# Two output norms: gain moved from the rows of W_out, and 1/rms from the accumulator add, onto the activations

## The chip, the cores and the metric

The kernel runs on one core of a Trainium2 chip. The metric is the device time of one execution in microseconds (us), the median of several. The core has a matrix engine (TensorE, PE in the rows; PEld is its weight load), VectorE (DVE), ScalarE (ACT), GpSimd (POOL) and SyncE (SP), which here only issues DMAs. PE writes to PSUM; the other compute engines read it, GpSimd excepted.

## The reference

```python
for i in range(DEPTH):                                     # DEPTH is 1
    proj = rmsnorm(h, norm_mix_g[i]) @ w_in[i]
    y_a = gmlp_chunk_mixer(proj[..., :GM_COLS], ...)       # ends: rmsnorm((u * mixed), gm_out_norm_g), width 1024
    y_b = ssd_mixer(proj[..., GM_COLS:], ...)              # ends: y * silu(z), then rmsnorm with ssd_norm_g,
                                                           #       two groups of 512 columns
    h = h + jnp.concatenate([y_a, y_b], axis=-1) @ w_out[i]
    hid = jax.nn.relu(rmsnorm(h, norm_mlp_g[i]) @ w_ff1[i])
    h = h + (hid * hid) @ w_ff2[i]
    gate = jax.nn.sigmoid(rmsnorm(h, ple_norm_g[i]) @ w_ple_gate[i])
    h = h + gate * (p[i] @ w_ple_proj[i])
return rmsnorm(h, final_norm_g)
```

x is 512 x 1024, everything is float32. The change touches the two rmsnorms that end `y_a` and `y_b`, and the product with `w_out` behind them.

## The kernel before

The 512 positions are four row tiles of 128. Every large product is made of three TensorE passes: both operands are split into a float32r high part and the rest (`w_hi`, `w_lo`, `a_hi`, `a_lo`, `b_hi`, `b_lo`), and high x high, high x low, low x high are added in PSUM. A weight block of 512 columns (or, for `w_out`, of four 128-row slices over all 1024 columns) arrives in `w_raw` by four DMAs of 512 KB from SyncE's queue, ACT rounds each piece to `w_hi` (L594), DVE subtracts to get `w_lo` (L989 or L991).

The first part runs through 36 steps t = 4 b + s: block b of `w_in` (v: 0, 1; the convolved columns: 2 to 4; u: 5, 6; z: 7, 8) against row tile s, 24 matmuls each. The order on each engine is written by hand as one loop over t, with semaphores between the engines, and work of other kinds is put at certain t. From t = 20 the state-space scan runs beside it, one unit j per two steps (j = 0 to 7, two groups of four chunks). Unit j needs: PE the product `cb` at odd t (L1615), DVE its mask and the product `lm` at even t (L1084, L1088), PE `off`, `diag` and `state` at even t (L1623, L1628, L1635), GpSimd the three products `xdt`, `xdd` and `y *= d_skip` after them (L541, L544, L548), then DVE at the following odd t the sum (L1151 to L1167). These small products go to four PSUM banks, `side`, filled in a fixed order. Bank 3 takes cb 6, off 6, cb 7, off 7: so `cb` of unit 7, which PE has behind its matmuls of t = 33, waits until DVE has read `off` of unit 6 in L1151, at t = 33 of DVE's own order.

`u * mixed` is multiplied in place in `h` (L1226, t = 20 to 27), its squares are summed by ACT (L791), and at t = 32 DVE takes the reciprocal of the rms (L1177, into `m_rstd`). PE turns `h` to `a_hi`/`a_lo` from t = 34 on (`yt` parts 0 and 1). `y * silu(z)` is multiplied in place in `y` (L1232, t = 28 to 35) and turned at t = 40 to 43 (`yt` parts 2 and 3).

The product with `w_out` is blocks OUT to OUT + 3 (b = 9 to 12, t = 36 to 51), 24 matmuls a tile into two PSUM banks, and DVE adds each finished tile to `h` (L1045), into which x has been read once more. Neither norm is applied to the activations: the gains of both norms are read as 16 rows of `rows`, turned to columns 68 to 83 of `cols`, and multiply the rows of `w_out` when it is split (L594 with `scale`, L989); `m_rstd` multiplies in the add (L1045), one column a row tile for y_a and for each group of y_b. After that come the PLE product, the feed-forward product (a seven-product scheme) and the gate.

The buffer `gain` has two slots of 1024 columns, each filled by a DMA that spreads a row of 4 KB over 128 partitions.

Of the kernel before, what the change touches and what calls it, by code (L numbers as in the profile page):

```python
# [5 lines left out]
P = 128  # L6
# [22 lines left out]
def build_layer(nc, a, out):  # L29
# [26 lines left out]
    with ExitStack() as ctx:  # L56
# [66 lines left out]
        rows = sb("rows", [P, P])  # L123
        cols = sb("cols", [P, 84])
        a_log = sb("a_log", [P, R])
# [66 lines left out]
        m_ssq_ready, m_rms_ready = sem("m_ssq_ready"), sem("m_rms_ready")  # L192
        m_rstd_ready = sem("m_rstd_ready")
        yt_hi, pt_hi = sem("yt_hi"), sem("pt_hi")
        f1_landed = [[sem(f"f1_landed{i}{p}") for p in range(2)] for i in range(3)]
# [140 lines left out]
        def _(sp):  # L336
# [38 lines left out]
            sp.dma_start(rows[60:68, :], a["gm_bs"][0]).then_inc(rows_landed, 16)  # L375
            sp.dma_start(rows[68:76, :], a["gm_out_norm_g"][0].rearrange("(i p) -> i p", p=P)).then_inc(rows_landed, 16)
            sp.dma_start(rows[76:84, :], a["ssd_norm_g"][0].rearrange("(i p) -> i p", p=P)).then_inc(rows_landed, 16)
            sp.dma_start(y[:, 0:1, :].rearrange("p a (g s) -> p (a g) s", g=GH),
# [9 lines left out]
            sp.wait_ge(xn_ready, NS)  # L388
            load_gain(a["norm_mlp_g"][0], 0)
            load_k(U, w_in, 0)  # L390
            load_k(U + 1, w_in, 512)
            for i in range(2):
                load_k(Z + i, w_in, 2 * W + 512 * i)
            load_rows(OUT, w_out, 0)
            load_rows(OUT + 1, w_out, 4)
            sp.wait_ge(m_ssq_ready, 4)
            for s in range(NS):
# [4 lines left out]
            sp.dma_start(tmp[:, 0:2, :].rearrange("p a (b n) -> p (a b) n", b=2), p_dram).then_inc(p_landed, 16)  # L402
            load_rows(OUT + 3, w_out, 12)
            for p in range(4):
                piece(PLE, p, w_ple[:, p // 2, 512 * (p % 2):512 * (p % 2) + 512], w_raw[:, p, 0, :])
# [175 lines left out]
        def _(act):  # L581
            def split_hi(b, p):

                half = b % 2 if b < GATE else 1 - b % 2
                act.wait_ge(w_landed[p], 16 * (b + 1))
                if b == GATE:
                    act.wait_ge(ff_step, product_end(UNITS - 1, "T4"))
                elif b > GATE:
                    act.wait_ge(ff_step, STEPS * UNITS)
                elif b >= 2:  # L590
                    act.wait_ge(acc_full, 4 * (b - 1))
                n = 1 if b == PLE else 2
                scale = cols[:, 68 + 4 * (b - OUT) + p:69 + 4 * (b - OUT) + p] if OUT <= b < PLE else 1.0
                act.activation(w_hi[:, half, 2 * p:2 * p + n, :], w_raw[:, p, 0:n, :], ACT.Copy, scale=scale  # L594
                               ).then_inc(hi_ready, 1)

# [382 lines left out]
        def _(dve):  # L979
            def split_lo(b, p):  # L980

                half = b % 2 if b < GATE else 1 - b % 2
                dve.wait_ge(hi_ready, 4 * b + p + 1)
                n = 1 if b == PLE else 2
                lo, raw = w_lo[:, half, 2 * p:2 * p + n, :], w_raw[:, p, 0:n, :]
                hi = w_hi[:, half, 2 * p:2 * p + n, :].bitcast(F32)
                if OUT <= b < PLE:
                    c = 68 + 4 * (b - OUT) + p
                    ins = dve.scalar_tensor_tensor(lo, raw, cols[:, c:c + 1], hi, ALU.mult, ALU.subtract)  # L989
                else:  # L990
                    ins = dve.tensor_tensor(lo, raw, hi, ALU.subtract)  # L991
                ins.then_inc(lo_ready, 1)

            def normed(n, s):

                i = 4 * n + s
                dve.wait_ge(rms_ready, i + 1)
                dve.reciprocal(rstd[:, i:i + 1], rms[:, i:i + 1]).then_inc(rstd_ready, 1)
                dve.wait_ge(rstd_ready, i + 1)
                slot, use = ((0, 1), (0, 2), (1, 2))[n]  # L1000
                c = s if n < 2 else TILES[s]
                if s == 0:
                    dve.wait_ge(gain_landed[slot], 16 * use)
                if n == 0:
                    dst = h[:, s, :]
                else:
                    dst = tmp[:, 2 * (s % 2):2 * (s % 2) + 2, :].rearrange("p a n -> p (a n)")
                dve.scalar_tensor_tensor(dst, h[:, c, :], rstd[:, i:i + 1], gain[:, slot, :], ALU.mult, ALU.mult
                                         ).then_inc(xn_ready, 1)
# [24 lines left out]
            def add_group(b, s):  # L1034

                dve.wait_ge(acc_full, 4 * b + s + 1)
                if b == OUT:
                    dve.wait_ge(x_landed[s], 32)
                else:
                    prev = before[b] + s + 1 - 4  # L1040
                    dve.wait_ge(dve_evac, prev)
                i = 2 * (s % 2)
                hs = h[:, s, :].rearrange("p (a n) -> p a n", a=2)
                c = 4 * max(b - OUT - 1, 0) + s
                dve.scalar_tensor_tensor(hs, acc[:, i:i + 2, :], m_rstd[:, c:c + 1], hs, ALU.mult, ALU.add  # L1045
                                         ).then_inc(dve_evac, 1)

# [43 lines left out]
            for t in range(4 * OUT):  # L1091
# [12 lines left out]
                if t == 3:  # L1104
                    bank = wait_full(dve, "cols")
                    freed(dve.tensor_copy(cols[:], bank[:, 0:84]), "cols")
                if t == 4:
# [67 lines left out]
                if t == 32:  # L1175
                    dve.wait_ge(m_rms_ready, 1)
                    dve.reciprocal(m_rstd[:, 0:4], m_rms[:, 0:4]).then_inc(m_rstd_ready, 1)  # L1177
                    dve.wait_ge(m_rstd_ready, 1)
                if t == 19:
                    mask_cb(0)  # L1180
# [53 lines left out]
            def yb_scale(g):  # L1234
# [3 lines left out]
                dve.reciprocal(m_rstd[:, at], m_rms[:, at]).then_inc(m_rstd_ready, 1)  # L1238
                dve.wait_ge(m_rstd_ready, 2 + g)


# [187 lines left out]
            for i in range(8):  # L1429
# [14 lines left out]
                if i == 0:  # L1444
                    dve.wait_ge(gain_landed[0], 16 * 3)
                dve.tensor_tensor(y[:, s, at], h[:, s, at], gain[:, 0, at], ALU.mult).then_inc(h_gain, 1)
# [11 lines left out]
        def _(pe):  # L1458
# [95 lines left out]
            for t in range(4 * OUT):  # L1554
# [5 lines left out]
                if t == 2:  # L1560
                    pe.wait_ge(rows_landed, 16 * 5)
                    filled(pe.transpose(open_bank("cols")[:, 0:84], rows[0:84, :], ident[0:84, 0:84]), "cols")
                if t == 4:
# [73 lines left out]
                if t >= 34:  # L1637
                    if t == 34:
                        pe.wait_ge(ya_mul, 8)
                    for k in (2 * (t - 34), 2 * (t - 34) + 1):  # L1640
# [3 lines left out]
            for b in range(OUT, OUT + 4):  # L1644
                for s in range(4):
# [14 lines left out]
                    if 40 <= t < 44:  # L1660
                        i = t - 40
                        pe.wait_ge(yb_mul, 5 + i)
                        for q in range(2):
# [131 lines left out]
```

## Time and profile before

| what | us |
|---|---|
| median of 3 runs | 754.24 |
| the runs | 754.21, 754.24, 755.58 |
| the profiled execution, device time | 755.58 |
| its span, first to last instruction | 753.8 |
| PE busy in it | 736.7 (98%) |
| DVE / ACT / POOL busy | 460.3 / 379.9 / 116.8 |

The profiled execution is the slowest of the three. In its rows, a matmul of 512 columns is shown with 0.39 us and the next begins 0.23 us after it, so a step of 24 takes about 5.5 us. Times of rows are us from the start of the span. A row's first number is its start, the second how long it took; "idle before" stands in brackets with what ended it.

### The profile page before, as it was taken

The numbers are of one execution on the slowest core, as the hardware profiler recorded it, in microseconds if no ns is written. First come the engines' busy times: TensorE is split into PE (matmuls) and PEld (weight loads), VectorE is DVE, ScalarE is ACT, GpSimd is POOL, SyncE is SP. The second block draws the span as 40 slices with busy tenths as digits, with TensorE's granted clock in tenths as the row PEclk, the third lists the DMA queues.
The fourth block names the chain that finished last, engine by engine and source line by source line (L and its number), as shares of the span: only waits on it lengthen the run. The fifth ranks groups of instructions, "written<-read, shape, count | busy, mean of one in ns | idle before, by whom it ended". The sixth has DMA issues, their size and how long they took to land.

```text
span 753.8 us, 8663 instructions
## 1 busy us (share of the span) xinstructions
PE 736.7 (98%) x3396; PEld 606.7 (80%) x3396; DVE 460.3 (61%) x492; ACT 379.9 (50%) x508; POOL 116.8 (15%) x92
## 2 busy tenths in 40 slices
PE   7999999999999999999999999999999999998896
PEld 7888877878878888888888888888888888886784
DVE  5557885576767465546454952586356844498854
ACT  5534456654674833314564523563257326554665
POOL 1021310766455000000002000110002000200000
PEclk9999999999999999999999999999999999999998
DMA  9632222352241163101967694477727681883311
GB/s 336 183 102 85 83 84 86 116 163 85 86 159 63 59 216 116 57 29 36 383 195 166 154 275 130 112 148 245 221 52 155 194 270 56 167 215 125 109 57 56
DMA packets 48001, 106.10 MB, mean 141 GB/s; under 512 B 4677, under 2 KB 6361, under 8 KB 47961
## 3 DMA queue, kind: packets, MB, share of 16 engines
q1 hardware_dynamic: 41096, 84.55, 33.5%
q0 software_dynamic: 5632, 16.78, 12.3%
q10 hardware_dynamic: 1232, 4.23, 1.9%
q8 instruction: 27, 0.44, 0.2%
q14 instruction: 14, 0.11, 0.0%
HBM read 88.73 MB, written 4.23 MB: 123 GB/s over the span
## 4 chain that ended last, share of the span: by engine, by line
PE 89%; DVE 7%; ACT 1%; issue 1%; DMA 1%; SPq 0%; DVEq 0%; ACTq 0%
PE acc L1469 26%; PE acc L1471 25%; PE acc L1470 25%; PE side L1531 3%; PE side L1628 2%; PE side L1470 1%; PE side L1471 1%; PE side L1469 1%; DVE ring_lo L1275 1%; DVE w_lo L991 1%; DVE h L1347 1%; PE side L1595 1%; DVE conv L1188 1%; DVE h L1332 1%; PE side L1635 1%
## 5 line engine op out<-in xcount | busy, mean ns | idle before, releaser
L1469 PE MATMUL acc<-w_hi,a_hi 128*128 128x512 f32 x256 | 104.3, 408 | 0.0
L1471 PE MATMUL acc<-w_hi,a_lo 128*128 128x512 f32 x256 | 100.0, 391 | 0.0
L1470 PE MATMUL acc<-w_lo,a_hi 128*128 128x512 f32 x256 | 99.7, 390 | 0.0
L1469 PE MATMUL acc<-b_hi,ring_hi 128*128 128x512 f32 x256 | 99.6, 389 | 0.0
L1470 PE MATMUL acc<-b_lo,ring_hi 128*128 128x512 f32 x256 | 99.6, 389 | 0.0
L1471 PE MATMUL acc<-b_hi,ring_lo 128*128 128x512 f32 x256 | 99.6, 389 | 0.0
L991 DVE TENSOR_TENSOR w_lo<-w_raw,w_hi 128x1024 fp32r<-128x1024 f32 (+1 forms) x48 | 67.2, 1409 | 31.7 <-ACT w_hi L594 31.3
L662 ACT ACTIVATE ring_hi<-quarter 128x1024 fp32r<-128x1024 f32 x56 | 56.5, 1051 | 51.1 <-PE acc L1471 31.4
L1275 DVE TENSOR_TENSOR ring_lo<-ring_raw,ring_hi 128x1024 fp32r<-128x1024 f32 x32 | 38.7, 1224 | 67.0 <-ACT ring_hi L662 66.8
L1275 DVE TENSOR_TENSOR ring_lo<-quarter,ring_hi 128x1024 fp32r<-128x1024 f32 x56 | 65.9, 1219 | 16.8 <-ACT ring_hi L662 16.8
L571 POOL DMA_DIRECT2D quarter<-quarter x24 | 20.8, 868 | 351.4 <-DMA quarter<-in_w_ff 223.7
L662 ACT ACTIVATE ring_hi<-ring_raw 128x1024 fp32r<-128x1024 f32 x32 | 33.8, 1057 | 60.3 <-DMA ring_raw<-in_w_ff 60.2
L1469 PEld LDWEIGHTS acc<-w_hi,a_hi 128*128 128x128 f32 x256 | 48.1, 188 | 10.8 <-issue 1.4
L1470 PEld LDWEIGHTS acc<-w_lo,a_hi 128*128 128x128 f32 x256 | 48.2, 188 | 10.7 <-issue 1.4
L1471 PEld LDWEIGHTS acc<-w_hi,a_lo 128*128 128x128 f32 x256 | 48.0, 188 | 10.4
L594 ACT ACTIVATE w_hi<-w_raw 128x1024 fp32r<-128x1024 f32 (+1 forms) x48 | 48.1, 1013 | 16.0 <-PE acc L1471 13.7
L1469 PEld LDWEIGHTS acc<-b_hi,ring_hi 128*128 128x128 f32 x256 | 48.1, 188 | 10.0
L1470 PEld LDWEIGHTS acc<-b_lo,ring_hi 128*128 128x128 f32 x256 | 48.1, 188 | 9.9
L1471 PEld LDWEIGHTS acc<-b_hi,ring_lo 128*128 128x128 f32 x256 | 48.1, 188 | 9.9
L1469 PE MATMUL acc<-w_hi,b_hi 128*128 128x512 f32 x128 | 50.6, 396 | 4.1 <-DVE b_lo L1020 4.1
L1471 PE MATMUL acc<-w_hi,b_lo 128*128 128x512 f32 x128 | 49.9, 390 | 0.0
L1470 PE MATMUL acc<-w_lo,b_hi 128*128 128x512 f32 x128 | 49.8, 389 | 0.0
(228 smaller groups left out, 1460.5 us busy)
## 6 DMA issues: line engine op xcount, KB each, us to landing
quarter<-in_w_ff SPq DMA_DIRECT2D x40, 512.0 KB, 4.8
w_raw<-in_w_in SPq DMA_DIRECT2D x36, 512.0 KB, 3.8
ring_raw<-in_w_ff SPq DMA_DIRECT2D x32, 512.0 KB, 5.4
quarter<-quarter POOLq DMA_DIRECT2D x24, 512.0 KB, 6.1
w_raw<-in_w_out SPq DMA_DIRECT2D x16, 512.0 KB, 3.5
h<-in_x SPq DMA_DIRECT2D x8, 512.0 KB, 4.4
seg<-cs_dram ACTq DMA_DIRECT2D x8, 512.0 KB, 3.8
quarter<-in_w_ff POOLq DMA_DIRECT2D x8, 512.0 KB, 6.6
```

The costliest lines, as they stand in the source:

```text
L571: pool.dma_start(quarter[QUARTER[name]][at], src, accum_op=ALU.add).then_inc(t_landed[QUARTER[name]][p], 16)
L594: act.activation(w_hi[:, half, 2 * p:2 * p + n, :], w_raw[:, p, 0:n, :], ACT.Copy, scale=scale).then_inc(hi_ready, 1)
L662: act.activation(hi[at], src, ACT.Copy).then_inc(form_hi, 1)
L991: ins = dve.tensor_tensor(lo, raw, hi, ALU.subtract)
L1188: ins = dve.scalar_tensor_tensor(dst, acc[:, s, 0:SEQ - k], w, dst, ALU.mult, ALU.add)
L1275: dve.tensor_tensor(lo[at], src, hi[at].bitcast(F32), ALU.subtract).then_inc(form_lo, 1)
L1332: dve.tensor_tensor(hq, hq, bank, op).then_inc(h_added, 1)
L1469: pe.matmul(dst, st[0], mv[0], start=start, stop=False)
L1470: pe.matmul(dst, st[0], mv[1], start=False, stop=False)
L1471: return pe.matmul(dst, st[1], mv[0], start=False, stop=stop)
L1531: ins = pe.transpose(bank[:, i * P:i * P + P], src(i), ident[:])
L1628: ins = pe.matmul(bank[:, r * HD:r * HD + HD], lm[:, r, :], xdt[:, r * HD:r * HD + HD], start=True, stop=True)
```

## The change

- The two gains are no longer read into `rows`; `cols` has 68 columns. W_out is split like every other weight: L594 without `scale`, a plain subtraction for `w_lo`.
- At t = 32, behind the reciprocal, DVE multiplies the four row tiles of `h` (1024 columns each) by 1/rms and gain, four new instructions, in place. It raises `ya_norm`; PE waits for it before it turns `h` at t = 34.
- At t = 37 and t = 39, in `yb_scale`, DVE does the same with four half tiles of `y` (512 columns) each, eight new instructions. They raise `yb_norm`; PE waits for it at t = 40 to 43.
- The add of a finished tile is a plain sum `h + acc`.
- SyncE's queue: gain slot 0 takes `gm_out_norm_g` where it took `norm_mlp_g`; slot 1 takes `ssd_norm_g` after a wait for `v_ready`, ahead of block U + 1; `norm_mlp_g` follows after a wait for `ya_norm`, ahead of block OUT + 1. The wait for `m_ssq_ready` ahead of the second read of x goes; the PLE pieces wait for `yb_norm`.

```diff
-            sp.dma_start(rows[68:76, :], a["gm_out_norm_g"][0].rearrange("(i p) -> i p", p=P)).then_inc(rows_landed, 16)
-            sp.dma_start(rows[76:84, :], a["ssd_norm_g"][0].rearrange("(i p) -> i p", p=P)).then_inc(rows_landed, 16)
...
             sp.wait_ge(xn_ready, NS)
-            load_gain(a["norm_mlp_g"][0], 0)
+            load_gain(a["gm_out_norm_g"][0], 0)
             load_k(U, w_in, 0)
+            sp.wait_ge(v_ready, NS)
+            load_gain(a["ssd_norm_g"][0], 1)
             load_k(U + 1, w_in, 512)
...
             load_rows(OUT, w_out, 0)
+            sp.wait_ge(ya_norm, NS)
+            load_gain(a["norm_mlp_g"][0], 0)
             load_rows(OUT + 1, w_out, 4)
-            sp.wait_ge(m_ssq_ready, 4)
...
-                scale = cols[:, 68 + 4 * (b - OUT) + p:69 + 4 * (b - OUT) + p] if OUT <= b < PLE else 1.0
-                act.activation(w_hi[:, half, 2 * p:2 * p + n, :], w_raw[:, p, 0:n, :], ACT.Copy, scale=scale
-                               ).then_inc(hi_ready, 1)
+                act.activation(w_hi[:, half, 2 * p:2 * p + n, :], w_raw[:, p, 0:n, :], ACT.Copy).then_inc(hi_ready, 1)
...
-                if OUT <= b < PLE:
-                    c = 68 + 4 * (b - OUT) + p
-                    ins = dve.scalar_tensor_tensor(lo, raw, cols[:, c:c + 1], hi, ALU.mult, ALU.subtract)
-                else:
-                    ins = dve.tensor_tensor(lo, raw, hi, ALU.subtract)
-                ins.then_inc(lo_ready, 1)
+                dve.tensor_tensor(w_lo[:, half, 2 * p:2 * p + n, :], w_raw[:, p, 0:n, :],
+                                  w_hi[:, half, 2 * p:2 * p + n, :].bitcast(F32), ALU.subtract).then_inc(lo_ready, 1)
...
-                c = 4 * max(b - OUT - 1, 0) + s
-                dve.scalar_tensor_tensor(hs, acc[:, i:i + 2, :], m_rstd[:, c:c + 1], hs, ALU.mult, ALU.add
-                                         ).then_inc(dve_evac, 1)
+                dve.tensor_tensor(hs, hs, acc[:, i:i + 2, :], ALU.add).then_inc(dve_evac, 1)
...
                     dve.wait_ge(m_rstd_ready, 1)
+                    dve.wait_ge(gain_landed[0], 32)
+                    for i in range(NS):
+                        dve.scalar_tensor_tensor(h[:, i, :], h[:, i, :], m_rstd[:, i:i + 1], gain[:, 0, :],
+                                                 ALU.mult, ALU.mult).then_inc(ya_norm, 1)
...
                 dve.wait_ge(m_rstd_ready, 2 + g)
+                dve.wait_ge(gain_landed[1], 32)
+                for i in range(NS):
+                    yv = y[:, i, 512 * g:512 * g + 512]
+                    dve.scalar_tensor_tensor(yv, yv, m_rstd[:, 4 + 4 * g + i:5 + 4 * g + i],
+                                             gain[:, 1, 512 * g:512 * g + 512], ALU.mult, ALU.mult).then_inc(yb_norm, 1)
...
-                        pe.wait_ge(ya_mul, 8)
+                        pe.wait_ge(ya_norm, NS)
...
-                        pe.wait_ge(yb_mul, 5 + i)
+                        pe.wait_ge(yb_norm, 5 + i)
```

VectorE at t = 32 and 33, before: the mask product of unit 6, the first piece of `w_out`, the reciprocal, the product with silu(z), the second piece, and the read of `off` (bank `side`).

```order
161 L1088 TENSOR_TENSOR lm<-lm,cbm 128x1024
162 L989 SCALAR_TENSOR_TENSOR w_lo<-w_raw,cols,w_hi 128x1024
163 L1177 RECIPROCAL m_rstd<-m_rms 128x4
164 L1232 TENSOR_TENSOR y<-y,tmp 128x512
165 L989 SCALAR_TENSOR_TENSOR w_lo<-w_raw,cols,w_hi 128x1024
166 L1151 TENSOR_TENSOR xs_t<-side,decay 128x512
```

The same stretch with the change (the lines have moved: L1144 is what L1151 was, L1229 what L1232 was).

```order
161 L1081 TENSOR_TENSOR lm<-lm,cbm 128x1024
162 L986 TENSOR_TENSOR w_lo<-w_raw,w_hi 128x1024
163 L1170 RECIPROCAL m_rstd<-m_rms 128x4
164 L1174 SCALAR_TENSOR_TENSOR h<-h,m_rstd,gain 128x1024 x4
165 L1229 TENSOR_TENSOR y<-y,tmp 128x512
166 L986 TENSOR_TENSOR w_lo<-w_raw,w_hi 128x1024
167 L1144 TENSOR_TENSOR xs_t<-side,decay 128x512
```

Four instructions of 1024 columns now stand between the reciprocal and everything up to the read of `off`.

VectorE at t = 37 to 40, before: adds of finished tiles, with the reciprocals of the y_b norm between them.

```order
188 L1045 SCALAR_TENSOR_TENSOR h<-acc,m_rstd,h 128x1024
189 L1238 RECIPROCAL m_rstd<-m_rms 128x4
190 L989 SCALAR_TENSOR_TENSOR w_lo<-w_raw,cols,w_hi 128x1024
191 L1045 SCALAR_TENSOR_TENSOR h<-acc,m_rstd,h 128x1024
```

With the change:

```order
189 L1039 TENSOR_TENSOR h<-h,acc 128x1024
190 L1235 RECIPROCAL m_rstd<-m_rms 128x4
191 L1240 SCALAR_TENSOR_TENSOR y<-y,m_rstd,gain 128x512 x4
192 L986 TENSOR_TENSOR w_lo<-w_raw,w_hi 128x1024
193 L1039 TENSOR_TENSOR h<-h,acc 128x1024
```

Four instructions of 512 columns come between the reciprocal and the next piece of weights; the same stands once more at t = 39.

## Rows read from the trace of the kernel before

**Rows 1.** The page: busy us by engine, and the granted clock in tenths by slice.

```profile
PE 736.7 (98%) x3396; PEld 606.7 (80%) x3396; DVE 460.3 (61%) x492; ACT 379.9 (50%) x508; POOL 116.8 (15%) x92
...
PEclk9999999999999999999999999999999999999998
```

**Rows 2.** Waits of PE: who for whom, us in total, times, longest us.

```profile
PE acc L1469 <- DVE b_lo L1020: 4.1, 2, 2.4
...
PE side L1531 <- ACT xs_t L833: 1.1, 2, 0.8
```

**Rows 3.** Timeline, DVE, 228 to 256 us: start, us, what.

```profile
235.26 0.17 DVE L1177 RECIPROCAL m_rstd<-m_rms 128x4 f32<-128x4 f32 x1
235.85 0.69 DVE L1232 TENSOR_TENSOR y<-y,tmp 128x512 f32<-128x512 f32 x1 [0.42 <-DVE m_rstd L1177]
236.84 1.28 DVE L989 SCALAR_TENSOR_TENSOR w_lo<-w_raw,cols,w_hi 128x1024 fp32r<-128x1024 f32 x1 [0.29 <-ACT w_hi L594]
238.04 0.68 DVE L1151 TENSOR_TENSOR xs_t<-side,decay 128x512 f32<-128x512 f32 x1
238.75 1.40 DVE L1156 TENSOR_TENSOR xs_t<-xs_t,y 128x512 f32<-128x512 f32 x1
...
240.79 0.81 DVE L1165 TENSOR_TENSOR carry<-carry,decay 128x512 f32<-128x512 f32 x1
241.64 0.69 DVE L1167 TENSOR_TENSOR carry<-side,carry 128x512 f32<-128x512 f32 x1
...
247.01 1.23 DVE L1088 TENSOR_TENSOR lm<-lm,cbm 128x1024 f32<-128x1024 f32 x1 [1.49 <-ACT lm L707]
```

**Rows 4.** Timeline, POOL, 222 to 256 us, the three instructions of unit 7.

```profile
238.56 1.04 POOL L541 TENSOR_TENSOR xdt<-y,dt 128x512 f32<-128x512 f32 x1 [6.42 <-PE side L1635]
239.68 1.37 POOL L544 TENSOR_TENSOR xdd<-xdt,decay 128x512 f32<-128x512 f32 x1
241.02 1.49 POOL L548 TENSOR_TENSOR y<-y,d_skip 128x512 f32<-128x512 f32 x1
```

**Rows 5.** Timeline, PE: `cb` and `diag` of unit 7, and the turn of `h`.

```profile
243.74 0.38 PE L1615 MATMUL side<-bcT 128*128 128x128 f32 x2
...
250.31 1.89 PE L1628 MATMUL side<-xdt,lm 128*128 128x64 f32 x16
252.04 1.04 PE L1531 MATMUL side<-ident,h 128*128 128x128 f32 x8
```

**Rows 6.** Timeline, DVE, 160 to 170 us, an instruction of 1024 columns beside POOL.

```profile
160.52 1.78 DVE L1088 TENSOR_TENSOR lm<-lm,cbm 128x1024 f32<-128x1024 f32 x1 [1.37 <-ACT lm L707]
```

**Rows 7.** Timeline, POOL, the instruction that ran beside it.

```profile
158.48 2.74 POOL L529 TENSOR_TENSOR seg<-seg,upper 128x1024 f32<-128x1024 f32 x1
```

**Rows 8.** Groups by line and form, DVE: busy us, mean ns, idle before.

```profile
L1008 DVE SCALAR_TENSOR_TENSOR tmp<-h,rstd,gain 128x1024 f32<-128x1024 f32 x8 | 10.3, 1284 | 0.3
...
L1188 DVE SCALAR_TENSOR_TENSOR conv<-acc,cols,conv 128x511 f32<-128x511 f32 x12 | 8.9, 745 | 10.1 <-ACT conv L824 10.1
```

**Rows 9.** Timeline, DVE, 272 to 290 us: adds and reciprocals.

```profile
273.39 0.17 DVE L1238 RECIPROCAL m_rstd<-m_rms 128x4 f32<-128x4 f32 x1
...
277.63 1.28 DVE L1045 SCALAR_TENSOR_TENSOR h<-acc,m_rstd,h 128x1024 f32<-128x1024 f32 x1 [2.75 <-PE acc L1471]
...
284.27 0.17 DVE L1238 RECIPROCAL m_rstd<-m_rms 128x4 f32<-128x4 f32 x1
...
288.52 1.28 DVE L1045 SCALAR_TENSOR_TENSOR h<-acc,m_rstd,h 128x1024 f32<-128x1024 f32 x1 [2.76 <-PE acc L1471]
```

**Rows 10.** Line L518, POOL, the product that raises `v_ready`: ns min/median/max, first and last start.

```profile
L518 POOL TENSOR_TENSOR h<-h,gain x4: 2389/2401/2402, 75.5 to 99.6; 128x1024 f32<-128x1024 f32 x4
```

**Rows 11.** Timeline, SP's queue: the last two weight pieces ahead of block U + 1.

```profile
114.00 5.57 SPq L341 DMA_DIRECT2D w_raw<-in_w_in  x2
```

**Rows 12.** Timeline, ACT, 222 to 345 us: the first split of block OUT + 1.

```profile
264.72 1.15 ACT L594 ACTIVATE w_hi<-w_raw,cols 128x1024 fp32r<-128x1024 f32 x1
```

**Rows 13.** DMA issues: KB each, us from issue to landing.

```profile
gain<-in_norm_mlp_g SPq DMA_DIRECT2D x1, 512.0 KB, 4.6
```

More of the change, by code:

```diff
@@ L123, in build_layer @@
         rows = sb("rows", [P, P])
-        cols = sb("cols", [P, 84])
+        cols = sb("cols", [P, 68])
         a_log = sb("a_log", [P, R])
@@ L193, in build_layer @@
         m_rstd_ready = sem("m_rstd_ready")
+        ya_norm, yb_norm = sem("ya_norm"), sem("yb_norm")
         yt_hi, pt_hi = sem("yt_hi"), sem("pt_hi")
@@ L403, in _ @@
             load_rows(OUT + 3, w_out, 12)
+            sp.wait_ge(yb_norm, 8)
             for p in range(4):
@@ L984, in split_lo @@
                 n = 1 if b == PLE else 2
-                lo, raw = w_lo[:, half, 2 * p:2 * p + n, :], w_raw[:, p, 0:n, :]
-                hi = w_hi[:, half, 2 * p:2 * p + n, :].bitcast(F32)
-                if OUT <= b < PLE:
-                    c = 68 + 4 * (b - OUT) + p
-                    ins = dve.scalar_tensor_tensor(lo, raw, cols[:, c:c + 1], hi, ALU.mult, ALU.subtract)
-                else:
-                    ins = dve.tensor_tensor(lo, raw, hi, ALU.subtract)
-                ins.then_inc(lo_ready, 1)
+                dve.tensor_tensor(w_lo[:, half, 2 * p:2 * p + n, :], w_raw[:, p, 0:n, :],
+                                  w_hi[:, half, 2 * p:2 * p + n, :].bitcast(F32), ALU.subtract).then_inc(lo_ready, 1)
             def normed(n, s):
@@ L999, in normed @@
                 dve.wait_ge(rstd_ready, i + 1)
-                slot, use = ((0, 1), (0, 2), (1, 2))[n]
+                slot, use = ((0, 1), (0, 3), (1, 3))[n]
                 c = s if n < 2 else TILES[s]
@@ L1105, in _ @@
                     bank = wait_full(dve, "cols")
-                    freed(dve.tensor_copy(cols[:], bank[:, 0:84]), "cols")
+                    freed(dve.tensor_copy(cols[:], bank[:, 0:68]), "cols")
                 if t == 4:
@@ L1444, in _ @@
                 if i == 0:
-                    dve.wait_ge(gain_landed[0], 16 * 3)
+                    dve.wait_ge(gain_landed[0], 16 * 4)
                 dve.tensor_tensor(y[:, s, at], h[:, s, at], gain[:, 0, at], ALU.mult).then_inc(h_gain, 1)
@@ L1560, in _ @@
                 if t == 2:
-                    pe.wait_ge(rows_landed, 16 * 5)
-                    filled(pe.transpose(open_bank("cols")[:, 0:84], rows[0:84, :], ident[0:84, 0:84]), "cols")
+                    pe.wait_ge(rows_landed, 16 * 3)
+                    filled(pe.transpose(open_bank("cols")[:, 0:68], rows[0:68, :], ident[0:68, 0:68]), "cols")
                 if t == 4:
```

## The prediction

> **What bounds the kernel now.** I read the page's busy times first. PE is busy 736.7 of 753.8 us [rows 1], and no other engine is over 61%. The list of what PE waited for is next: its largest entry is 4.1 us near the end, the others are smaller, and the view of 110 to 690 us alone lists none (the largest, and the last one ahead of the changed stretch: [rows 2]). So an edit elsewhere is worth something only where it makes PE wait or takes a wait of PE away; a wait that PE gets is added whole, since behind it PE again has no idle time that could take it up. The granted clock is full in all slices but the last [rows 1], and those waits of up to 2.4 us have not lowered it, so a wait of a few us costs only itself. The change adds work to VectorE at two places. I therefore took from the timeline how far ahead of PE VectorE is there.
>
> **What goes, and what gets cheaper.** Two DMAs of 4 KB at the start, and 16 of 84 columns in one turn by PE: no entry of PE's waits names `rows`, so 0. The 16 splits of `w_out` and the 16 adds change from the three-operand form to the two-operand form. An instruction of 1024 columns takes 1.28 us in the first form (L989, L1045) and 1.23 us in the second (L1088) [rows 3, 9]: 32 x 0.05 = 1.6 us of VectorE, all beside matmuls, since PE waits for none of them. On the path: 0. ACT's split without a scale, the same: 0.
>
> **The DMAs.** Three gain rows are spread where one was. One took 4.6 us to land [rows 13]. The new wait for `v_ready` stands ahead of block U + 1. The last of the four products that raise it starts at 99.6 and takes 2.4 us [rows 10], so it is there at 102.0; the queue comes to the wait only after the last piece of block U, which it issues after 114 us [rows 11]. Cost 0. The wait for `ya_norm` holds the pieces of block OUT + 1 until VectorE has done the four products of `h`, at about 241 us by the sum below; behind it are one gain transfer and then those pieces. They are first read by ACT at 264.72 [rows 12], over 20 us later, against some 10 us for two transfers of this size. Cost 0; it would begin to cost if `ya_norm` came after about 254. The second read of x waits for turns of PE as before, and PLE's pieces for an event that is long past.
>
> **The y_b products, t = 37 and 39.** Each time four instructions of 512 columns. The nearest row in that form has 511 columns and takes 0.745 us [rows 8], and instructions that stand back to back begin some 0.08 us before the end of the one ahead (236.84 + 1.28 against 238.04) [rows 3]: 4 x 0.67 = 2.7 us. The first reciprocal ends at 273.56; products to 276.3; the piece of weights to 277.5; the add that then follows starts at 277.63 when PE has finished its tile [rows 9]. It is covered with 0.1 us to spare, and the bank that the add frees is not opened again by PE until a tile of 5.5 us later. The second: 284.44 + 2.7 + 1.2 = 288.3 against 288.52 [rows 9]. PE wants the first turned half tile at the same 288.5, and its product is ready at 285.2. Cost 0 for both. With that cover gone, PE would still have some 4 us on the bank. GpSimd is idle in this stretch.
>
> **The y_a products, t = 32: the term that counts.** Four instructions of 1024 columns. The same form with the same operands takes 1.284 us [rows 8], one every 1.20: 4.8 us on VectorE. The turn of `h` that needs them is at 252.04 [rows 5], so that wait is covered by 11 us. But they also stand ahead of L1151, the read of `off` 6, which frees PSUM bank 3 for `cb` 7. Before, L1151 ended at 238.72 [rows 3], and PE opened the bank at 243.74 [rows 5]: a lead of 5.0 us. The plain sum uses up nearly all of it. The reciprocal moves to 235.2, the products start at 235.4, 236.6, 237.8 and 239.0, the product with silu(z) (whose input ACT has ready at 235.8) starts at 240.2, the weight piece at 240.8, and L1151 runs from 242.0 to 242.6. That is 1.1 us ahead of PE.
>
> GpSimd takes that lead away. At 238.56 it starts its three instructions of unit 7 [rows 4]. The rows show that it and VectorE take turns where both read their operands from SBUF. L1156 starts at 238.75, inside L541 (to 239.60), and lasts 1.40 us in place of 0.69: it ends 0.55 after L541. L544, begun at 239.68, ends 0.90 after L1156's end at 240.15. L1165 ends 0.55 after L544 (241.05), and L548, already begun, 0.91 after L1165 (241.60) [rows 3, 4]. An instruction of 1024 columns ends 1.08 after GpSimd's (162.30 against 161.22) [rows 6, 7]. L1151, which reads PSUM, takes 0.68 beside L541 and is not held [rows 3].
>
> With the products in place the order of arrival gives: third product ends 239.10; L541, waiting since 238.56, to 240.00; fourth product (1.15 after it) to 241.15; L544 to 242.05; the product with silu(z) to 242.60; L548 to 243.50; the weight piece, 1.08, to 244.6; L1151 from 244.5 to 245.2. PE starts `cb` 7 at 245.2 and not at 243.74: **1.5 us** of waiting. Bounds of this term: 0 below, where VectorE keeps its lead of 1.1 us (PE has then no wait that could shrink), and about 2.3 above (next part).
>
> As to who goes first, L1165, waiting since 240.79, got in ahead of L548 although L548 begins 0.03 before L544 ends [rows 3, 4]: the one that waits longer wins against the one that follows on its own engine. The reverse, GpSimd getting in between two instructions of VectorE that stand back to back, has no row of its own. Nor is there a row in which the three-operand form reads two operands from SBUF beside GpSimd. I take the order of arrival for both, since that is what the nearest rows do.
>
> On the second point a page speaks. The Trainium skill, "SBUF — State Buffer", section "SBUF: two separate sides", says that VectorE and GpSimd share a port pair under an exclusive lock for the whole instruction, and that any VectorE instruction with two SBUF inputs takes it against a GpSimd one that reads SBUF. That includes the new products. By that rule the sum is the 1.5 us above; without it, 0.2 us (below). It speaks against this change, and the rows of the two-operand form agree with it.
>
> Behind the wait nothing more is late. `diag` 7 follows `cb` 7 after 6.57 us (250.31 - 243.74) [rows 5]. From L1151's end to L1167's end VectorE took 3.6 us (238.72 to 242.33), after it come products of 0.69, 0.28 and 1.23 us: 5.8 us [rows 3]. That leaves 0.8 us.
>
> **The sum.** For the profiled execution 755.58 + 1.5 = 757.1, with a span of 755.3. It is 1.3 us above the median of the runs, which is the number to compare: 754.24 + 1.5 = 755.7. A measurement of this kernel can tell about 0.2%, 1.5 us, from no change, so the forecast lies on that border.
>
> **Rivals.**
> *No wait.* VectorE's back-to-back products are not interrupted: GpSimd waits until 242.0, L1151 ends at 242.6, and PE finds the bank free: 754.2. Or the three-operand form isn't held: GpSimd runs L541 and L544 to 240.7, the product with silu(z) ends at 241.3, L548 at 242.2, the weight piece at 243.3, L1151 at 243.9: a wait of 0.2, 754.4. For it: no row shows either; against it: how L1165 and L548 take turns. Chance 0.22.
> *A second wait, clearly slower.* GpSimd's turns slip behind the weight piece, so that L1156 and L1165 are held as they were before, and `lm` of unit 7 comes after PE is ready for `diag` 7. It decides from a VectorE chain of 6.6 us between L1151's end and `lm`, 0.8 above my sum; a slip of one or two turns (0.9 each) brings 0.1 to 1 us on top of 1.5: some +2.3 in all, 756.5. Against it: L548 is through by 243.5. Chance 0.12.
> *Something gained.* The 1.6 us saved on VectorE would have to be on PE's path, and PE waits for none of those instructions: 0.03, and some 0.03 for what I don't see.
>
> **How the numbers follow.** Forecast 0.60, at 755.7, with 755.3 to 756.1 for the size of the turns; half of it is over the border of 755.75. Slower by over 0.2%: 0.30 + 0.12 + 0.01 = 0.43. Faster by over 0.2%: 0.04. The same: 0.53. The range takes in no wait at all, with 0.2 for the runs' own spread, and the second wait with its upper end: 754.0 to 757.0. Outside it is 0.1.
>
> **What would show it.** In the profile after: four products L1174 from 235.4 us with the fourth longer than 1.28 (about 2.1 us), GpSimd's first instruction near 238.56 with about 1.4 us, L1144 (which was L1151) ending near 245.2, and a PE wait of 1.5 us at `cb` 7, named as VectorE's read of `off`. Wrong: four products of 1.28 each with GpSimd's first instruction 3 us or longer (VectorE keeps the ports), or no wait of PE there; a PE wait between 270 and 300 us; or a wait at `diag` 7.

## The result and the profile after

The changed kernel takes 758.43 us (median of 6 runs, 757.68 to 759.0) against 754.32 of the kernel before: a ratio of 1.0051, interval 1.0038 to 1.0064. That is 4.1 us slower, where 1.5 were forecast and 757.0 was the upper end. The six runs fall in two groups of three, at 757.7 to 757.9 and at 758.9 to 759.0, and the median is the middle between them. In a second series of 10 runs it is 757.76 against 755.68, a ratio of 1.0024 (1.0007 to 1.0041).

The times of both kernels fall on a few levels, groups of runs within a few tenths of a us of each other. The lowest level of before is 754.2, that of the changed kernel 756.1 (once in 16 runs); its usual levels are 757.7 and 759. So two questions stand: where 1.9 us between the lowest levels come from, and why the changed kernel is so rarely on its lowest.

What PE waited for in the changed kernel (to be laid beside [rows 2]):

```profile
PE acc L1471 <- DVE b_lo L1015: 4.1, 2, 2.4
...
PE side L1533 <- DVE tmp L1003: 1.3, 1, 1.3
PE side L1617 <- DVE xs_t L1144: 1.3, 1, 1.3
```

The last line is new: it is the forecast wait at `cb` 7. The line above it is the turn near 692 us, 0.9 us in the kernel before. The timeline of VectorE around t = 32 answers to [rows 3]:

```profile
235.80 5.66 DVE L1174 SCALAR_TENSOR_TENSOR h<-h,m_rstd,gain 128x1024 f32<-128x1024 f32 x4
241.39 1.53 DVE L1229 TENSOR_TENSOR y<-y,tmp 128x512 f32<-128x512 f32 x1
242.84 2.06 DVE L986 TENSOR_TENSOR w_lo<-w_raw,w_hi 128x1024 fp32r<-128x1024 f32 x1
244.82 0.68 DVE L1144 TENSOR_TENSOR xs_t<-side,decay 128x512 f32<-128x512 f32 x1
```

and that of GpSimd to [rows 4]:

```profile
238.96 1.42 POOL L544 TENSOR_TENSOR xdt<-y,dt 128x512 f32<-128x512 f32 x1 [6.42 <-PE side L1637]
240.46 1.91 POOL L547 TENSOR_TENSOR xdd<-xdt,decay 128x512 f32<-128x512 f32 x1
242.33 1.49 POOL L551 TENSOR_TENSOR y<-y,d_skip 128x512 f32<-128x512 f32 x1
```

Everything in this profile is 0.4 us later than in before's from the first turn on, since the first gain row happened to land that much later; with 0.4 taken off, each row is within 0.2 us of the sum. Four products end at 241.46 (241.15 + 0.4 in the sum), GpSimd's instructions take 1.42, 1.91 and 1.49 (1.44, 1.97 and 1.40), L1144 ends at 245.50 (245.2 + 0.4). PE answers to [rows 5]:

```profile
243.91 0.39 PE L1473 MATMUL acc<-w_hi,a_lo 128*128 128x512 f32 x1
245.55 0.49 PE L1617 MATMUL side<-bcT 128*128 128x128 f32 x2 [1.25 <-DVE xs_t L1144]
245.80 0.48 PE L1471 MATMUL acc<-w_hi,a_hi 128*128 128x512 f32 x1
```

where before had

```profile
243.51 0.39 PE L1471 MATMUL acc<-w_hi,a_lo 128*128 128x512 f32 x1
243.74 0.38 PE L1615 MATMUL side<-bcT 128*128 128x128 f32 x2
243.88 0.48 PE L1469 MATMUL acc<-w_hi,a_hi 128*128 128x512 f32 x1
```

From the last matmul ahead of `cb` to `cb` it is 1.64 us where it was 0.23: a wait of 1.4 us. To the first matmul behind `cb` it is 1.89 us where it was 0.37, so PE has lost 1.5 us in all. What the sum did not have stands at the end. PE's rows behind its wait for `b_lo`, before:

```profile
698.21 0.47 PE L1469 MATMUL acc<-w_hi,b_hi 128*128 128x512 f32 x1 [2.35 <-DVE b_lo L1020]
698.52 0.40 PE L1470 MATMUL acc<-w_lo,b_hi 128*128 128x512 f32 x1
698.75 0.40 PE L1471 MATMUL acc<-w_hi,b_lo 128*128 128x512 f32 x1
698.99 0.40 PE L1469 MATMUL acc<-w_hi,b_hi 128*128 128x512 f32 x1
```

and after:

```profile
700.49 0.47 PE L1471 MATMUL acc<-w_hi,b_hi 128*128 128x512 f32 x1 [2.35 <-DVE b_lo L1015]
700.80 0.48 PE L1472 MATMUL acc<-w_lo,b_hi 128*128 128x512 f32 x1
701.07 0.63 PE L1473 MATMUL acc<-w_hi,b_lo 128*128 128x512 f32 x1
701.50 0.63 PE L1471 MATMUL acc<-w_hi,b_hi 128*128 128x512 f32 x1
701.92 0.63 PE L1472 MATMUL acc<-w_lo,b_hi 128*128 128x512 f32 x1
```

The wait is the same 2.35 us. After it the matmuls follow at 0.43 us in place of 0.23. The view by stretches gives the clock: the columns are the stretch, its length, then busy us of PE, PEld, DVE, ACT and POOL, the granted clock as a share, DMA share, GB/s. First the changed kernel, then before.

```profile
701.00:704.00 3.00, 3.00 (x8) 2.34 (x7) 2.96 (x5) 1.44 (x3) 0.00 (x0) 0.50 0.52 182
```

```profile
698.30:701.60 3.30, 3.30 (x17) 2.73 (x18) 3.27 (x5) 1.45 (x3) 0.00 (x0) 1.00 0.58 207
```

TensorE ran at 1.2 GHz after the wait in the one and at 2.4 GHz in the other: 8 matmuls in 3 us against 17 in 3.3.

Taken apart, the profiled executions differ by 3.8 us of span. The turn is where PE turns `tmp` (L1531, L1533) near 692 us; the step is the time from the start of the matmul ahead of it to its start; the tail is the time from its start to the end.

| part of the span | before | after | more |
|---|---|---|---|
| to the first matmul of the first product | 12.4 | 12.8 | 0.4 |
| from the last matmul ahead of `cb` 7 to the first behind it | 0.37 | 1.89 | 1.5 |
| step of PE to its turn near 692 | 1.33 | 1.69 | 0.4 |
| tail, from that turn to the end | 61.8 | 63.3 | 1.5 |

### The profile page after: what moved, and what is told of

Same layout as the page of the kernel before. It is cut to its first block, busy times and chain, and to the rows that moved or that the text cites. A ratio compares the mean times of both kernels' runs of the same rounds, so it can differ in the third digit from the quotient of the medians.

```text
span 757.6 us, 8676 instructions
## 1 busy us (share of the span) xinstructions
PE 738.5 (97%) x3396; PEld 607.7 (80%) x3396; DVE 470.8 (62%) x504; ACT 378.4 (50%) x508; POOL 117.8 (16%) x92
## 4 chain that ended last, share of the span: by engine, by line
PE 87%; DVE 8%; issue 2%; ACT 2%; DMA 1%; SPq 0%; DVEq 0%; ACTq 0%
PE acc L1471 25%; PE acc L1473 25%; PE acc L1472 25%; PE side L1533 3%; PE side L1630 2%; PE side L1473 1%; PE side L1471 1%; PE side L1472 1%; DVE w_lo L986 1%; DVE ring_lo L1277 1%; DVE h L1349 1%; PE side L1597 1%; DVE conv L1185 1%; DVE h L1334 1%; DMA gain<-in_norm_mix_g 1%
## 5 line engine op out<-in xcount | busy, mean ns | idle before, releaser
L986 DVE TENSOR_TENSOR w_lo<-w_raw,w_hi 128x1024 fp32r<-128x1024 f32 (+1 forms) x64 | 88.5, 1390 | 32.0 <-ACT w_hi L596 31.4
L596 ACT ACTIVATE w_hi<-w_raw 128x1024 fp32r<-128x1024 f32 (+1 forms) x64 | 64.8, 1026 | 34.1 <-PE acc L1473 31.3
```

The costliest lines, as they stand in the source:

```text
L986: dve.tensor_tensor(w_lo[:, half, 2 * p:2 * p + n, :], w_raw[:, p, 0:n, :], w_hi[:, half, 2 * p:2 * p + n, :].bitcast(F32), ALU.subtract). ...
```

## Experiments

**The changed kernel again.** No edit.

> The changed kernel once more, for a second trace. What the first trace shows over the kernel before: PE starts its first turn 0.4 us later (DMA of the first gain row), waits 1.4 us at cb 7, waits 0.4 us longer at 694 us, and runs 15 matmuls at the 1.2 GHz clock behind its wait of 2.7 us near 698 us, 1.5 us more. Theory A (all but the first are fixed by the program): the wait at cb 7 of 1.4 us, the 0.4 us at 694 and the stretch at 1.2 GHz come again; 757.6 to 759. Theory B (the low clock and the 0.4 us are chance of one execution): cb 7 alone comes again, and the median of this series is near 755.8.

Measured: lowest 756.08, then six runs at 757.6 to 757.8 and three at 759.1 to 759.2. In the trace the wait at `cb` 7, the longer step to the turn (1.68) and the tail of 63.3 us are there again. The start is another: the clock is full from 6.8 us on, the first product begins at 11.0 us where it was 12.8 in the first trace of this kernel and 12.4 in before's, and the span is 756.0. So theory A holds, but for its claim on the low clock: one run of ten, at 756.08, is shorter than wait and turn with a low clock behind them would allow. 756.08 - 754.21 = 1.87, and the first two terms are 1.5 + 0.4 = 1.9. The stretch behind the wait, in the second trace:

```profile
699.80:703.00 3.20, 3.20 (x9) 2.43 (x9) 3.16 (x4) 1.36 (x3) 0.00 (x0) 0.50 0.62 200
```

**The y_a products spread.** `ya_scale(i)` is the product of one row tile, as in the block that it replaces.

```diff
+                if t == 34:
+                    ya_scale(2)
                 if t >= 22 and t % 2 == 0:
                     mask_cb((t - 20) // 2)
...
                 if t == 32:
...
-                    for i in range(NS):
-                        dve.scalar_tensor_tensor(h[:, i, :], h[:, i, :], m_rstd[:, i:i + 1], gain[:, 0, :],
-                                                 ALU.mult, ALU.mult).then_inc(ya_norm, 1)
+                if t == 33:
+                    ya_scale(0)
+                    ya_scale(1)
+                if t == 34:
+                    ya_scale(3)
```

> The four y_a products are not in one block at t = 32: two stand at the end of t = 33 (behind the carry), one at the start of t = 34, one behind the third weight piece of t = 34, where VectorE had idle time. All else as in the changed kernel. By the theory of the ports and the full order on VectorE: the read of off 6 is at 238.1 again, PE has no wait at cb 7, 1.4 us less. If the low clock near 701 us hangs on where PE's wait near 698 us falls, it goes too, and the time is 754.6 (0.4 us left at 694). If the low clock comes from the products themselves or from the longer queue of DMAs, it stays: 756.2. If the wait at cb 7 is not from the block of products, nothing changes: 757.7 or more.

Measured: lowest 754.65, median 756.05 (before 755.68; ratio 1.0002, 0.9987 to 1.0017), one run of ten at 757.7. Its timeline of VectorE:

```profile
237.88 0.68 DVE L1151 TENSOR_TENSOR xs_t<-side,decay 128x512 f32<-128x512 f32 x1
...
241.50 3.27 DVE L1086 SCALAR_TENSOR_TENSOR h<-h,m_rstd,gain 128x1024 f32<-128x1024 f32 x2
...
245.30 1.27 DVE L1086 SCALAR_TENSOR_TENSOR h<-h,m_rstd,gain 128x1024 f32<-128x1024 f32 x1
...
249.38 1.28 DVE L1086 SCALAR_TENSOR_TENSOR h<-h,m_rstd,gain 128x1024 f32<-128x1024 f32 x1
```

The read of `off` is back at 238, and PE has no wait at `cb` 7. The same four products, the same gain rows and DMAs, the same y_b products, and 1.4 us less at the lowest level: the wait came from the block of products ahead of L1144. The low clock is gone from the trace (1.00 in the stretch of 3.3 us behind the wait), and the usual level fell by 1.7 (from 757.75 to 756.05). The product that runs beside GpSimd's last instruction is again the longer one (3.27 for two).

**PE later by its own work, without the change.**

```diff
                 banks_free(b, s)
+                if 4 * b + s == 34:
+                    for i in range(8):
+                        pe.matmul(acc[:, s, :], a_hi[:, 0, 0:P], w_hi[:, 0, 0, :], start=True, stop=True)
```

> The kernel before with 8 matmuls of 512 columns added on PE ahead of the product of t = 34 (into the bank that this product then starts anew; the result is not used). It has none of the change, only a PE that is 1.84 us later from 244 us on (8 x 0.23). If the low clock hangs on when the wait near 698 us falls: a stretch at 1.2 GHz behind it as in the changed kernel, 1.84 + 1.5 = 3.3 us slower, 757.6. If the low clock is a matter of the change itself: 1.84 us slower, 756.1.

The other kernel is the same with `range(15)`.

> The same with 15 added matmuls, 3.45 us of PE work. If the low clock hangs on when the wait near 698 us falls, and a still later one is again harmless: 3.4 us slower, 757.7, no slower than with 8 added. If a later wait always gets the low clock: 3.4 + 1.5 = 4.9 us slower, 759.2. If the clock has nothing to do with it: 3.4 us slower and the kernel with 8 added is 1.8 us slower.

Measured: with 8 added 757.61 at the lowest, five runs of ten there and five at 759.0 to 759.3, median 758.45; with 15 added 757.63 at the lowest, four there and six at 759.1 to 759.5, median 759.09 (the medians count how many runs fell on each level). Between the lowest times 7 matmuls, 1.6 us of work, cost nothing. The lowest times can be added up: with 15, 754.2 + 3.45 = 757.65, so these runs had no low clock at the end; with 8, 754.2 + 1.84 = 756.05, which none of ten runs reached, and 1.5 more is 757.6. The stretches of the two kernels behind the same wait of 2.35 us, 8 added first:

```profile
699.80:703.10 3.30, 3.30 (x9) 2.53 (x8) 3.27 (x4) 1.35 (x3) 0.00 (x0) 0.50 0.55 184
```

```profile
702.00:705.40 3.40, 3.32 (x17) 2.78 (x18) 3.37 (x5) 1.45 (x3) 0.00 (x0) 1.00 0.73 223
```

The tail is 63.4 us with 8 and 61.8 with 15. A kernel with nothing of the change gets the low clock from being 1.84 us later, and no longer has it when it is 3.4 us later. So the low clock is not made by the norm products or the DMAs. It depends on when that wait falls, and the 1.9 us of the change move it to a place where nearly every run meets it. Which times are bad, and what they are counted from, these runs do not show.

**The place in VectorE's list.**

```diff
             dve.memset(eps[:], EPS).then_inc(eps_ready, 1)
+            for i in range(13):
+                dve.memset(spare[:, i:i + 1], 0.0)
```

> The kernel before with 13 instructions more on VectorE at its very start (13 memsets of one column, about 0.8 us, in its 4.6 us of idle time there). VectorE's list is then as much longer ahead of 686 us as with the change, and nothing else is changed. Theory of the place in the list: the 0.4 us between the two sums h22 - h21 and h22 + h12 near 685 us, and PE's wait for its turn near 691 us of 1.3 in place of 0.95 us, come as in the changed kernel; lowest time 754.6 in place of 754.2. Rival, that these 0.4 us come from the changed work (adds in two-operand form, other DMAs): PE's wait stays at 0.95.

Measured: lowest 754.58 and six of ten runs there to 754.76; PE's step to its turn is 1.68 us, as in the changed kernel, and the sums near 685 us show why:

```profile
681.80 1.23 DVE L1350 TENSOR_TENSOR h<-h 128x1024 f32<-128x1024 f32 x1
683.48 1.23 DVE L1350 TENSOR_TENSOR h<-h 128x1024 f32<-128x1024 f32 x1 [0.46 <-DVE h L1350]
```

**Further down the list.** The kernel with the products spread, and 30 such memsets.

> The kernel with the y_a products spread, with 30 memsets of one column more at VectorE's start: VectorE's list is longer still. Theory of the place in the list: the 0.4 us are no longer between those two sums, PE's wait for its turn near 691 us is 0.95 us again, lowest time 754.3. Rival, that they come from the changed work: 1.3 us and 754.65 as with the products spread alone.

Measured: lowest 754.19, four of ten runs to 754.31 and six at 755.4 to 755.7, median 755.47; the step is 1.33. The two sums stand together again, 2.55 us for both:

```profile
681.70 2.55 DVE L1361 TENSOR_TENSOR h<-h 128x1024 f32<-128x1024 f32 x2
```

Thirteen instructions more, some 680 us earlier on the same engine and in its idle time, put 0.4 us between two dependent sums; thirty more on top of the change take it out. It is the number of instructions ahead, not what they do. The Trainium skill, "Runtime: NRT & Kernel Launch", section "Instruction fetch mechanics", says that instructions come in blocks, fetched ahead, with the cost of a border mostly hidden. The traces agree as to the place. Counted with its semaphore instructions, the sum behind the gap is VectorE's 576th in the traces with the gap, the 563rd in before's and the 606th with the 30 memsets. The packets of the trace hold instruction transfers of 8 KB; those that move when nothing but VectorE's list grows start, in before's, when VectorE is at its 192nd, 318th, 445th and 573rd instruction. The last of them starts at 693.27 us in before's trace, at 684.16 with the 13 memsets, which is 0.7 us behind the start of the sum behind the gap, at 685.42 and again 0.7 us behind it in the kernel with the products spread, and at 660.61 with 30 memsets more. A border of blocks just ahead of the 576th instruction fits all of these. That VectorE waits there for the fetch, and why it shows between these two sums, no run shows; this part of the cause stays open.

**Filling PE's wait, too long and then to measure.** 18 small matmuls, then 9, ahead of the gate product.

```diff
+                if i == 0:
+                    for _ in range(18):
+                        pe.matmul(acc[:, 0, 0:P], ident[:], ones[:], start=True, stop=True)
                 if b == 0:
                     for q in range(2):
                         wait_free(pe, ("xt", 2, j, q))
```

> The changed kernel with 18 small matmuls (128 columns, constants, result not used) on PE right ahead of the gate product, where it waits 2.35 us for b_lo near 698 us. They take 18 x 0.11 = 2.0 us of that wait, and PE starts the gate product at the same time. If the low clock there comes from the idle time: no stretch at 1.2 GHz behind it, tail of 61.8 us behind the turn near 692 us in place of 63.35; 1.5 us off the median, 756.1 to 757.5 in place of 757.8. If it does not come from the idle time: nothing changes.

Measured: 757.5 to 759.0, no gain, tail 63.2 us. The profile shows 36 records where I had counted 18:

```profile
696.45 4.18 PE L1757 MATMUL acc<-ones,ident 128*128 128x128 f32 x36
700.38 0.48 PE L1471 MATMUL acc<-w_hi,b_hi 128*128 128x512 f32 x1
```

They took 4.2 us, and the gate product began 1.4 us late (7.6 us behind the start of the turn in place of 6.2). The matmuls behind it follow at 0.23, so the clock was full, but what that gave back the filling had used up. The same holds for the other kernel with 18.

> Both: the y_a products spread, and the 18 small matmuls ahead of the gate product. No wait at cb 7 and no low clock behind the wait near 698 us in any run; what is left over the kernel before is the 0.4 us near 691. 754.65 where the clock is full early at the start, 756.0 where it is full late, and no run at 757.7; a tie with the kernel before or a little faster in the median, since that kernel has runs with the low clock too.

Measured: 756.04 to 756.23 in five runs, 757.1 to 757.5 in five: 1.4 us above the kernel with the products spread, a plain miss of my size. With 9 in the changed kernel:

> The changed kernel with 9 small matmuls ahead of the gate product in place of 18: in the profile each is two records of 0.11 us, so 18 took 4.0 us and PE started the gate product 1.6 us late; 9 take 2.0 us of a wait of 2.35. If the low clock behind it comes from the idle time: none, tail 61.8 us behind the turn, lowest time 756.1 in many runs and no run above 757.6 (those are the runs whose clock rises late at the start). If 2.0 us of work there is no help: times as of the changed kernel, 757.7 and 759.2 in nearly all runs.

Measured: 755.80 to 756.06 in five runs and 757.2 to 757.5 in five; median 756.62 against 755.61 of before, ratio 1.0018 (1.0007 to 1.0029). The tail is 61.6 us, and the levels above 757.6 are gone. Behind the wait:

```profile
699.00:702.30 3.30, 3.30 (x21) 2.77 (x19) 3.27 (x5) 1.45 (x3) 0.00 (x0) 1.00 0.71 201
```

With the idle time filled the low clock does not come, so it needs that idle time as well as the bad moment. The same 9 matmuls in the kernel before give what the change costs without it.

> The kernel before with the same 9 matmuls. Its runs lie at 754.3, 755.7, 757.2 and 758.7. If the steps above 755.7 are low clock behind that wait: only 754.3 and 755.7 are left. If they have another cause: they stay.

Measured: four runs at 754.07 to 754.42, six at 755.3 to 755.75, none above; in the same series the kernel before had 3 of 35 at 757.1 or more, in the other two series 7 and 7 of 31. Few runs, but the direction is the expected one. Level for level (755.8 to 756.1 against 754.1 to 754.4, 757.2 to 757.5 against 755.3 to 755.75) the changed kernel is 1.7 to 1.8 us slower: the wait at `cb` 7 and the longer step.

**The start as well.**

```diff
-            for i in range(WARM):
+            for i in range(WARM + 4):
                 pe.matmul(acc[:, i % 2, 0:P], ident[:], ones[:], start=True, stop=True)
             turn_norm(0, 0)
```

> As fill9_before, and the first row of small matmuls at PE's start is 14 long in place of 10, so that PE is busy from 1.7 us until near the first turn at 7.8 us, where it had 1.9 us of idle time. If the two levels 754.3 and 755.7 come from a clock that rises at 6 to 7 us in some runs and at 11.4 us in others because of that idle time: most runs at 754.3. If the clock rises late all the same: both levels stay; if the longer row delays the first turn: all runs later by up to 0.5 us.

Measured: all 12 runs between 754.06 and 754.36; median 754.21 against 755.61 of before, ratio 0.9985 (0.9977 to 0.9994). The first stretch, before and then with the longer row:

```profile
6.00:11.40 5.40, 3.68 (x18) 3.69 (x19) 3.94 (x5) 3.50 (x5) 0.00 (x0) 0.68 1.04 404
```

```profile
6.00:11.40 5.40, 4.38 (x39) 4.14 (x38) 3.69 (x5) 3.50 (x5) 0.00 (x0) 1.00 1.04 404
```

The two levels 1.4 us apart that both kernels have come from this start. Before's own trace shows how: PE had a wait of 2.15 us, and behind it the clock was at 1.2 GHz (0.50) until 11.4 us, after it had been full (1.00 from 4.6 to 7.9 us).

```profile
7.72 1.76 PE L1531 MATMUL side<-ident,h 128*128 128x128 f32 x8 [2.15 <-DVE h L1008]
```

```profile
4.60:7.90 3.30, 1.15 (x11) 0.96 (x10) 1.45 (x2) 1.12 (x4) 0.00 (x0) 1.00 0.96 336
8.00:11.40 3.40, 3.40 (x18) 3.40 (x17) 2.66 (x4) 3.14 (x5) 0.00 (x0) 0.50 1.04 410
```

With the longer row the wait is 1.02 us and no such stretch follows.

> The changed kernel with all four causes taken away: the y_a products spread (no wait at cb 7), 30 memsets at VectorE's start (no 0.4 us near 691), 9 small matmuls ahead of the gate product and 14 at the start (clock). If these are the whole of what the change cost, it ties with warm_before, most runs at 754.3. If something of the change is still unexplained (the y_b products, the longer DMA queue, the longer VectorE list), it is slower than warm_before by that.

Measured: all 11 runs between 754.03 and 754.36, median 754.15. It ties with `warm_before` (754.21), and nothing of the change is left unexplained: the y_b products, the three gain rows and the longer list cost nothing that these runs can tell. Both are faster than the two kernels of this study, and the gain is the clock's, not the change's.

## Why the prediction was wrong

**What was right.** The place, the size and the mechanism of the forecast term: 1.4 us at `cb` 7, by turns of VectorE and GpSimd, with each of their rows within 0.2 us of the sum (1.5 in the sum, a wait of 1.4 and 0.1 for the matmuls behind it in the trace). The two points for which no row stood are settled. The three-operand form with both operands in SBUF is held by GpSimd and holds it (the four products took 5.66 us where 4 x 1.20 is 4.8; three took 1.28 and the one that GpSimd held 2.07), and GpSimd gets in between two instructions of VectorE that stand back to back (L544, waiting since 238.96, ran to 240.38 between the third and the fourth). The first of the two is as the Trainium skill, "SBUF — State Buffer", section "SBUF: two separate sides", has it, and the trace agrees: 1.4 us, not the 0.2 of the rival without the lock. That an instruction which reads PSUM is not held rested on L1151, which began before GpSimd did; [rows 3] and [rows 4] have a better one, L1167, with 0.69 us in the middle of L548. The second wait at `diag` 7 did not come. The y_b products were covered with as little to spare as worked out; in the changed kernel the add starts 0.22 us after the piece of weights:

```profile
275.45 2.74 DVE L1240 SCALAR_TENSOR_TENSOR y<-y,m_rstd,gain 128x512 f32<-128x512 f32 x4
278.11 1.22 DVE L986 TENSOR_TENSOR w_lo<-w_raw,w_hi 128x1024 fp32r<-128x1024 f32 x1
279.55 1.22 DVE L1039 TENSOR_TENSOR h<-h,acc 128x1024 f32<-128x1024 f32 x1 [0.22 <-PE acc L1473]
```

The DMAs, the removed ones and the cheaper forms together cost and gave 0 within what the runs can tell, as said (`warm_spread` against `warm_before`).

**The step that failed** is the one in the first paragraph: "those waits of up to 2.4 us have not lowered it, so a wait of a few us costs only itself". It is false in its second half. The wait that was added did not lower the clock; but it moved an old wait of 2.35 us near 698 us, harmless in before's trace, to a time where it does: 1.5 us more, shown by the kernels with 8 and 15 added matmuls and taken away by filling that wait. One trace in which a wait is harmless does not say that it is harmless when shifted by 1.9 us. No rival had this.

The first half is false too, and before's trace showed it: behind the wait of 2.15 us that ends at 7.72 us the clock is at 1.2 GHz until 11.4 us. The row of the page from which "full in all slices but the last" was read has a 9 there. A 9 is 90% or more: before's first slice of 18.85 us has a mean of 0.91 and is shown as 9, and so is the slice of the changed kernel that holds its low stretch. A low stretch of this length shows only in a view of shorter stretches.

**A smaller term** was missing altogether: 0.4 us on VectorE's chain to the turn near 692 us. I had counted the twelve products by what they hide behind at t = 32 to 39 and not by what a longer list does to a chain 400 to 450 us later. The view would not have shown it; the runs with 13 and with 30 memsets do.

**The range** allowed 0.2 us for the runs' own spread and had no term for the 1.3 us between 754.21 and 755.58. They are two levels, by a clock that is full from 6 to 7 us on or only from 11 to 12 us on, and before's profile was one of the upper level. The forecast term alone gives 757.1 on that level, which is above the range already. Had I read that, the clock would have stood among the causes. The total is 1.5 + 0.4 between the lowest levels, and 1.5 for the low clock in most runs: 3.4, which leads from 754.3 to 757.7, the lower of the two usual levels of the changed kernel; the upper is the start's 1.3 above it. In the first series five of six runs of before were on its lowest level and half of the changed kernel's on its upper: that they fell so was luck, and it makes 4.1 of 3.4.

## What to carry to other kernels

A block of VectorE work with both operands in SBUF costs more than its own time where GpSimd works too; put it into VectorE's idle slots, one or two instructions each, and follow it to the next read that frees a PSUM bank for PE. Where TensorE waits 2 us and more, as at both places here, ask not only what a change adds to the wait but where it moves it: the clock behind it can fall, for 1.5 us; a row of small matmuls that ends before the wait does kept it up here. Do not take a 9 in the page's clock row for a full clock. Compare the lowest times and the levels of two kernels as well as their medians.

## What the runs showed of the hardware

- After a wait of 2.35 us, PE ran at 1.2 GHz (0.43 us a matmul of 512 columns against 0.23) with 8 added matmuls 450 us earlier and at 2.4 GHz with 15: the time at which the wait fell decided. With 2.2 us of it filled by small matmuls the clock stayed full.
- Behind a wait of 2.15 us at 7.7 us the granted clock went from 1.00 to 0.50 until 11.4 us; with that wait at 1.02 us it stayed full, and twelve of twelve runs were on the lowest level.
- 13 instructions more at VectorE's start put 0.4 us between two dependent instructions near 685 us; 30 more than the change took them away. Instruction transfers of 8 KB come 126 to 128 VectorE instructions apart, and the gap lies just ahead of the 576th.
- VectorE's product of 1024 columns with two SBUF operands took 2.07 us in place of 1.28 when GpSimd's turn came ahead of it.
- A float32 matmul of 128 columns is two records of 0.11 us in the profile, so 18 of them keep PE busy for 4.2 us.
